# A decoder trunk's down projection as seven block products in three phases between the feed-forward tiles

## The reference, cut to what matters

```python
    x = layer_norm(ALPHA * x + merged @ w_out, ln1_g, ln1_b)
    f = (jax.nn.silu(x @ w_ff_gate) * (x @ w_ff_up)) @ w_ff_down
    x = layer_norm(ALPHA * x + f, ln2_g, ln2_b)
```

## Time and profile before

| what | value |
|---|---|
| three runs | 937.16, 937.13, 936.77 us; median 937.13 |
| span of the profiled execution | 935.2 us |
| TensorE busy | 921.6 us (99%) in 7307 matmuls |
| VectorE, ScalarE, GpSimd busy | 709.8, 423.3, 258.3 us |
| feed-forward quads | 575 to 786 us |
| down projection | 786 to 924 us |

### The profile page before, as it was taken

The page is one execution under the profiler, slowest core; times in us unless marked ns, Lnnn a source line. Parts: engine busy times, 40 slices in busy tenths (PEclk is TensorE's granted clock), DMA queues, the critical chain, the costliest instruction groups (busy, mean ns, idle before and its releaser), DMA issues.

```text
span 935.2 us, 18698 instructions
## 1 busy us (share of the span) xinstructions
PE 921.6 (99%) x7307; PEld 918.0 (98%) x7307; DVE 709.8 (76%) x1063; ACT 423.3 (45%) x682; POOL 258.3 (28%) x230
## 2 busy tenths in 40 slices
PE   9999999999999999999999999999999999999995
PEld 8999999999999999999999999999999999999995
DVE  2899999899869889877877699987878878321126
ACT  4422232326667534555544357555554557222223
POOL 4666565658200000000006441000000004443324
PEclk9999999999999999999999999999999999999998
DMA  8633233313436434432333321433334333422202
GB/s 237 193 88 86 84 100 90 89 58 91 144 115 220 164 111 115 114 88 83 108 102 113 94 66 47 120 106 90 90 95 123 96 90 104 145 86 85 79 2 96
DMA packets 169413, 98.29 MB, mean 105 GB/s; under 512 B 4954, under 2 KB 165506, under 8 KB 169361
## 3 DMA queue, kind: packets, MB, share of 16 engines
q1 hardware_dynamic: 167129, 96.66, 35.4%
q10 hardware_dynamic: 2232, 0.92, 0.4%
HBM read 89.94 MB, written 7.62 MB: 104 GB/s over the span
## 4 chain that ended last, share of the span: by engine, by line
PE 94%; DVE 3%; POOL 1%; DMA 1%; issue 0%; ACT 0%; SPq 0%; POOLq 0%; DVEq 0%
PE main L1323 49%; PE main L1484 27%; PE aux L1484 5%; PE aux L1323 4%; PE main L1556 4%; PE aux L1556 1%; PE main L1748 1%; PE aux L1309 1%; DMA x_tok<-in_x_prompt 1%; PE main L1359 1%; POOL r_tok L760 1%; DVE merged L2244 1%; DVE main L2241 0%; POOL r_tok L762 0%; DVE aux L2255 0%; PE aux L1699 0%
## 5 line engine op out<-in xcount | busy, mean ns | idle before, releaser
L644 POOL TENSOR_TENSOR w_lo<-raw,w_hi 128x1024 fp32r<-128x1024 f32 (+1 forms) x70 | 166.7, 2385 | 627.9 <-ACT w_hi L774 620.8
L774 ACT ACTIVATE w_hi<-raw 128x1024 fp32r<-128x1024 f32 x127 | 133.8, 1057 | 149.5 <-PE main L1323 114.9
L1323 PE MATMUL main<-x_hi,w_lo 128*128 128x272 f32 x752 | 155.8, 288 | 0.0
L1323 PE MATMUL main<-x_hi,w_hi 128*128 128x272 f32 x752 | 155.6, 288 | 0.0
L1323 PE MATMUL main<-x_lo,w_hi 128*128 128x272 f32 x752 | 155.1, 288 | 0.0
L1323 PEld LDWEIGHTS main<-x_hi,w_lo 128*128 128x128 f32 x752 | 118.1, 188 | 0.0
L1323 PEld LDWEIGHTS main<-x_lo,w_hi 128*128 128x128 f32 x752 | 118.1, 188 | 0.0
L1323 PEld LDWEIGHTS main<-x_hi,w_hi 128*128 128x128 f32 x752 | 117.4, 189 | 0.0
L1874 DVE SCALAR_TENSOR_TENSOR aux<-glu_pad,miscT,aux 128x512 f32<-128x512 f32 x112 | 75.1, 748 | 0.0
L2229 DVE SCALAR_TENSOR_TENSOR scr<-x_lo,main 128x544 f32<-128x544 f32 x6 | 4.3, 722 | 86.9 <-PE main L1323 86.9
L1323 PE MATMUL main<-y,w_hi 128*128 128x272 f32 x384 | 63.6, 287 | 0.0
(11 more groups left out here) (438 smaller groups left out, 2670.6 us busy)
## 6 DMA issues: line engine op xcount, KB each, us to landing
raw<-in_w_in SPq DMA_DIRECT2D x63, 512.0 KB, 4.2
raw<-in_w_ff_gate SPq DMA_DIRECT2D x22, 512.0 KB, 4.0
raw<-in_w_ff_up SPq DMA_DIRECT2D x22, 512.0 KB, 5.1
raw<-in_w_branch SPq DMA_DIRECT2D x32, 256.0 KB, 3.5
raw<-in_w_ff_down SPq DMA_DIRECT2D x16, 512.0 KB, 3.9
raw<-in_w_out SPq DMA_DIRECT2D x8, 512.0 KB, 3.9
raw<-in_w_ff_down SPq DMA_DIRECT2D x8, 384.0 KB, 3.3
kept_sums<-g_made_hi SPq DMA_DIRECT2D x4, 544.0 KB, 3.5
```

Of the source, the lines that this page charges most:

```text
L644: pool.tensor_tensor(w_lo[s][:, 0:n, :], raw[s][:, 0:n, :], w_hi[s][:, 0:n, :].bitcast(F32), ALU.subtract).then_inc(w_lo_ready, 1)
L774: act.activation(w_hi[s][:, :, :], raw[s][:, :, :], ACT.Copy).then_inc(w_hi_ready, 1)
L1323: mm = pe.matmul(ps[:, h, :], w[s][:, k, :], x[:, h * HALF:(h + 1) * HALF], start=(first and k == 0 and j == 0), stop=(last and k == n - 1 ...
```

## The change

The down projection is no longer a stage of its own. The 22 hidden chunks are taken as 11 pairs, in three phases of 4, 4 and 3 pairs. After the feed-forward quads 0 to 6 come four steps of phase 0 ("down", 0, o), after 7 to 14 four of phase 1, after 15 to 19 the last phase (list STEPS, 33 steps; step s in what follows is its index: 0 to 6, 7 to 10, 11 to 18, 19 to 22, 23 to 27, and 28 to 32 at the end). A down step makes two output tiles (2o and 2o + 1) from the pairs of its phase by the same seven products as a feed-forward quad: 4 chunks x 3 = 12 matmuls in each product of phases 0 and 1, 9 in phase 2. The blocks are a11, a12, a21, a22 of the hidden tiles (second index: even or odd chunk; first: rows 272 to 543 or 0 to 271) and their sums s1 to s4. In phase 2 only tiles 0 to 5 are done so; tiles 6 and 7 ("plain", steps 28 and 32) take 6 chunks x 3 x 2 matmuls each.

GpSimd makes for every pair the four sums (hid_sum) and the seven low parts (hid_low; eight in phase 2), each an operation of 272 columns, in the step after the pair is complete (steps 0, 2, 4, 6, 12, 14, 16, 18, 24, 26, and 27 and 28 for the last). ScalarE makes the high parts (hid_high) between its other work. The partial outputs are kept in merged, which ScalarE first scales by ALPHA (scale_x1, after steps 1 to 4): in every down step GpSimd adds the old value to each kept part (add_rows), VectorE's add_11, add_12 and add_22 write back to merged, and add_21 is a new one. The residual is thereby already in; the two operations of residual become one for the plain tiles (add_plain, residual_last) and none for the others. GpSimd no longer makes the low parts of the weights, except four in the last steps; VectorE does. The hardware loops over quads are written out flat. SP loads each tile of w_ff_down in two transfers and brings ln2_g and ln2_b ahead of the weights of step 31. Tiles are transposed in the order 6, 1, 0, 3, 2, 5, 4, 7.

The core of the diff (SP, GpSimd, ScalarE, TensorE, VectorE in turn):

```diff
+FIRST_PAIR, PAIRS = (0, 4, 8), (4, 4, 3)
+STEPS = ([("ff", q) for q in range(7)] + [("down", 0, o) for o in range(4)]
+         + [("ff", q) for q in range(7, 15)] + [("down", 1, o) for o in range(4)]
+         + [("ff", q) for q in range(15, KF - 2)] + [("plain", KD - 2)]
+         + [("down", 2, o) for o in range(3)] + [("plain", KD - 1)])
+S_LAST = len(STEPS) - 1
+S_PLAIN, S_END = STEPS.index(("plain", KD - 2)), STEPS.index(("down", 2, 2))
...
+            for s in range(S_LAST + 1):
+                kind, p = STEPS[s], s % 2
+                if s < 2:
+                    sp.wait_ge(w_lo_ready, U_FF + 2 * s + 2)
+                else:
+                    sp.wait_ge(left_lo_ready, s - 1)
+                    sp.wait_ge(right_lo_ready, quads(s - 2))
+                    sp.wait_ge(t4_ready, quads(s - 2))
+                if s == S_END:
+                    sp.wait_ge(p7_done, quads(S_PLAIN))
+                    for dst, name in ((g_row, "ln2_g"), (b_row, "ln2_b")):
+                        sp.dma_start(dst[:, :], i_[name].to_broadcast([P, D])).then_inc(row_vecs, 16)
...
-            with pool.Fori(0, KD // 4) as i:
-                for j in range(12):
-                    lo(i * 12 + (U_DOWN + j), j % RING, DOWN_SPLIT[j % 3])
...
+                a, b, op = {"s1": ("a21", "a22", ALU.add), "s2": ("s1", "a11", ALU.subtract),
+                            "s3": ("a11", "a21", ALU.subtract), "s4": ("a12", "s2", ALU.subtract)}[part]
...
+                pool.tensor_tensor(hid_f(part, ph, j), hid_f(a, ph, j), hid_f(b, ph, j), op)\
+                    .then_inc(hid_sum_ready, 1)
...
+            def pair_sums(ph, j):
+
+                both_made(ph, j, 0)
+                both_made(ph, j, 1)
+                hid_sum(ph, j, "s1")
+                hid_sum(ph, j, "s2")
+                hid_sum(ph, j, "s3")
+                hid_low(ph, j, "a11", "s3")
+                if ph == 2:
+                    hid_low(ph, j, "a21", "s3")
+                hid_sum(ph, j, "s4")
+                hid_low(ph, j, "s1", "s2")
+                hid_low(ph, j, "a12", "s4")
+                hid_low(ph, j, "s2", "s4")
+                hid_low(ph, j, "s3")
+                hid_low(ph, j, "s4")
+                hid_low(ph, j, "a22", "s1")
+
+            def add_rows(s):
+
+                if s == step_of("down", 0, 0):
+                    pool.wait_ge(x1_scaled, KD // 2)
+                for kept, rdy, where in ((kept_1, kept_1_ready, "11"), (kept_5, kept_5_ready, "22"),
+                                         (kept_2, kept_2_ready, "12")):
+                    pool.wait_ge(rdy, sums_to(s))
+                    pool.tensor_tensor(kept[:, :], kept[:, :], rows_of(s, where), ALU.add).then_inc(kept_added, 1)
...
+            for ph in range(2):
+                for j in range(PAIRS[ph]):
+                    pair_sums(ph, j)
+                for o in range(4):
+                    add_rows(step_of("down", ph, o))
+            pair_sums(2, 0)
+            pair_sums(2, 1)
+            both_made(2, 2, 0)
+            hid_sum(2, 2, "s3")
+            hid_low(2, 2, "a11")
+            hid_low(2, 2, "a21")
+            tile_made(KF - 1, 0)
+            hid_low(2, 2, "a12")
+            hid_low(2, 2, "s3")
+            tile_made(KF - 1, 1)
+            hid_sum(2, 2, "s1")
+            hid_sum(2, 2, "s2")
+            hid_low(2, 2, "s1", "s2")
+            hid_low(2, 2, "a22", "s1")
+            hid_sum(2, 2, "s4")
+            hid_low(2, 2, "s2", "s4")
+            hid_low(2, 2, "s4")
+            right_low(S_PLAIN + 2)
+            add_rows(S_PLAIN + 1)
+            left_low(S_PLAIN + 3)
+            right_low(S_PLAIN + 3)
+            add_rows(S_PLAIN + 2)
+            left_low(S_LAST)
+            add_rows(S_PLAIN + 3)
...
+                pair = pair_of(s - 1) if s else (0, 0)
+                left_high(s + 1)
+                keep_1(s)
+                if is_quad(s + 1):
+                    sum_high(s + 1, 0)
+                keep_5(s)
+                if is_quad(s + 1):
+                    right_high(s + 1)
+                if pair:
+                    hid_high(*pair, "a11")
+                    if pair[0] < 2:
+                        hid_high(*pair, "a12")
+                if is_ff(s - 1):
+                    silu_2(s - 1)
+                if is_quad(s + 1):
+                    sum_high(s + 1, 1)
+                keep_2(s)
+                if pair and pair[0] == 2:
+                    hid_high(*pair, "a21")
+                    hid_high(*pair, "a12")
+                if pair:
+                    hid_high(*pair, "a22")
+                    hid_high(*pair, "s1")
+                if is_quad(s + 1):
+                    sum_high(s + 1, 2)
+                if is_ff(s):
+                    silu_1(s)
+                if pair:
+                    hid_high(*pair, "s2")
+                    hid_high(*pair, "s3")
+                    hid_high(*pair, "s4")
...
+            for s in range(S_PLAIN - 1):
+                step(s)
+                if 1 <= s <= KD // 2:
+                    scale_x1(2 * s - 2)
...
+            s = S_PLAIN
+            left_high(s + 1)
+            hid_high(2, 2, "a12")
+            sum_high(s + 1, 0)
+            right_high(s + 1)
+            sum_high(s + 1, 1)
+            silu_2(s - 1)
+            hid_high(2, 2, "s1")
+            hid_high(2, 2, "a22")
+            hid_high(2, 2, "s2")
+            sum_high(s + 1, 2)
+            hid_high(2, 2, "s4")
             act.wait_ge(bn_zero, 1)
             act.activation(bn_rs[:, 0:1, 0:1], bn_mv[:, 0:1, 1:2], ACT.Sqrt, bias=EPS)
...
+            s = S_PLAIN + 1
+            keep_1(s)
+            keep_5(s)
+            left_high(s + 1)
+            sum_high(s + 1, 0)
+            right_high(s + 1)
+            keep_2(s)
+            sum_high(s + 1, 1)
+            sum_high(s + 1, 2)
...
+            for s in range(S_PLAIN):
+                product_1(s)
+                product_5(s)
+                if s:
+                    product_4(s - 1)
+                product_6(s)
+                product_2(s)
+                product_3(s)
+                product_7(s)
+
+            s, f0 = S_PLAIN, 2 * FIRST_PAIR[2]
+            pe.wait_ge(left_lo_ready, s + 1)
+            pe.wait_ge(hid_lo_ready, made(lo_order, 2, 1, "a22"))
+            for f in range(f0, f0 + 4):
+                first_plain(f, first=(f == f0))
+            product_4(s - 1)
+            pe.wait_ge(hid_lo_ready, made(lo_order, 2, 2, "a21"))
+            first_plain(f0 + 4)
+            s = S_PLAIN + 1
+            product_1(s)
+            product_2(s)
+            product_5(s)
+            pe.wait_ge(hid_lo_ready, made(lo_order, 2, 2, "a22"))
+            first_plain(f0 + 5, last=True).then_inc(plain_done, 1)
+            product_6(s)
+            product_3(s)
+            product_7(s)
...
+            def add_21(s):
+
+                rows_ = rows_of(s, "21")
+                ve.wait_ge(p4_done, quads(s))
+                ve.tensor_tensor(rows_, bank_of(s, "a"), rows_, ALU.add).then_inc(c21_ready, 1)
...
+            s = S_PLAIN + 1
+            two_sums(s + 1)
+            third_sum(s + 1)
+            sum_low(s + 1, 0)
+            add_11(s)
+            last_sum(s + 1)
+            sum_low(s + 1, 1)
+            left_low(s + 1)
+            add_plain()
+            sum_low(s + 1, 2)
+            add_12(s)
```

More of the change, by code:

```diff
@@ L257, in build @@
                 ("up_1", "up_2", "gate_1", "gate_2", "kept_1", "kept_2", "kept_5")))
[L259 to L274 removed]
+        HB = HALF * 4
@@ new lines, in made, with is_ff, is_quad, quads @@
+        def made(order, ph, j, part):
+            done = 0
+            for ph_ in range(ph + 1):
+                for j_ in range(PAIRS[ph_] if ph_ < ph else j):
+                    done += len(order(ph_, j_))
+            return done + order(ph, j).index(part) + 1
+        def is_ff(s):
+            return 0 <= s and STEPS[s][0] == "ff"
+        def is_quad(s):
+            return 0 <= s and STEPS[s][0] != "plain"
+        def quads(s):
+            return sum(is_quad(t) for t in range(s + 1))
@@ new lines, in scale_x1, with pair_of @@
+            def scale_x1(m):
+                if m == 0:
+                    act.wait_ge(x_sum_ready, 4)
+                    act.wait_ge(x1_lo_ready, 2 * KD)
+                part = merged[:, m:m + 2, :]
+                act.activation(part, part, ACT.Copy, scale=ALPHA).then_inc(x1_scaled, 1)
+            def pair_of(s):
+                if not is_ff(s) or STEPS[s][1] % 2 == 0:
+                    return None
+                g = STEPS[s][1] // 2 + 1
+                ph = sum(g >= k0 for k0 in FIRST_PAIR) - 1
+                return ph, g - FIRST_PAIR[ph]
@@ new lines, in _ @@
+            s = S_PLAIN + 1
+            keep_1(s)
+            keep_5(s)
+            left_high(s + 1)
+            sum_high(s + 1, 0)
+            right_high(s + 1)
+            keep_2(s)
+            sum_high(s + 1, 1)
+            sum_high(s + 1, 2)
+            s = S_PLAIN + 2
```

(51 more changed lines are left out.)

933 lines of the change are left out of this document (517 added, 416 removed).

## The result

The changed kernel takes 952.59 us (median of 4 runs, 951.73 to 954.0), the kernel before 937.14 (4 runs): 1.0167 times, with a 95% interval of 1.0153 to 1.0182. Forecast were 957 and slower. The profiled execution has a span of 952.2 us, 17.0 more than before.

A forecast was written before the change was run, and what follows sets the result against it. TensorE was taken to bound the feed-forward and down projection, but not the end. Span 935.2 less 1.8 (saving left after the end part) plus 22.0 (turns) gave 955.4; with 1.9 to the runs' median, 957 us, range 936 to 970.

The forecast's parts named there:

- The saving: Down projection: 933 matmuls instead of 1056, 123 fewer at 0.1255 us each, 15.4 us less.
- The edits at nothing: Weight transfers, row vectors, scale_x1, flat loops and VectorE's work in down steps were all priced at no cost.
- The turns: GpSimd and two-SBUF-input VectorE operations alternate, each turn costing VectorE about 0.6 us; 22.0 us in all.
- phase 0: Cost of GpSimd turns in this phase: 4.4 + 1.6 + 1.6 + 3.6 = 11.2 us, the 4.4 at step 0.
- phase 1: Cost of GpSimd turns in this phase: 0.3 + 1.6 + 1.6 + 3.6 = 7.1 us.
- the steps to the end of 27: Phase 2's turns: 0.9 for its first pair, 1.3 for ScalarE's s3 copy waiting before keep_2; 2.2 us.
- Rival D: Feed-forward and down steps: half the GpSimd and VectorE turns collide, costing 11 us, giving 946; chance 0.23.
- The Trainium skill's rule: A two-SBUF-input VectorE operation and a GpSimd operation hold a shared port pair exclusively; the other fully blocks.
- The end part: After product 7 of step 27: waits sum to 7.2 us; without the lock the saving of 15.4 becomes 1.8.
- C: ScalarE becomes the bound: s4 late from GpSimd delays keep_1 before product 6, 14 us on top, 971; chance 0.17.
- A: The lock hardly bites, only the end part costs: 935.3, on the edge between faster and the same; chance 0.10.
- B: The saving arrives, the end part's waits absent too: 921.7, or 929.5 with half of it; chance 0.10.

The follow-up runs named there:

- e1: The changed kernel with the sums and low parts of ten of the eleven pairs moved from GpSimd to VectorE: 941.46 us, 1.0044.
- b_two: The kernel before plus 114 GpSimd subtractions of two 128x272 SBUF tiles in the feed-forward, onto a scratch tile: 948.87 us, 1.0122.
- b_set: The kernel before plus 114 GpSimd memsets of a 128x272 scratch tile in the feed-forward: 938.36 us, 1.0012.
- all: The changed kernel with every pair on VectorE, pair (0,0) one step later, square root behind rows(4), steps 29 and 30 reordered: 934.96 us, 0.9976.
- all3: all with the last stretch reordered, three waits mended and the last four weight parts moved from GpSimd to VectorE: 930.61 us, 0.9928.

## Why the forecast was right, and where its numbers were off

**The saving** is as counted: 7307 matmuls before, 7184 after, 123 less, and where nothing waits 72 of them take 9.04 us as in the earlier trace rows.

**The edits at nothing.** No wait of TensorE behind 575 us names a transfer. scale_x1 did cost, though no wait names it. ScalarE before product 6 of step 3, which waited 1.02 us for keep_1 (the last row):

```profile
613.77 0.43 ACT L1420 ACTIVATE x_hi<-h_f 128x272 fp32r<-128x272 f32 x1 [1.13 <-POOL h_f L888]
614.10 1.10 ACT L1428 ACTIVATE merged<-merged 128x1088 f32<-128x1088 f32 x1
...
616.05 0.38 ACT L1383 ACTIVATE kept<-main 128x272 f32<-128x272 f32 x1
```

The second row is scale_x1, between a hid_high that waited for GpSimd's s4 and keep_1. Step 5 has the same order and waits 0.93. In phase 1 the pairs come the same way, without scale_x1, and product 6 waits nowhere. No run takes scale_x1 out by itself.

**The turns** are shown, not only argued: GpSimd subtractions alone lengthen VectorE's two-input operations in the kernel before, memsets do not, and taking the pairs off GpSimd gives 11.1 us back. The size was too large. The sum had 20.5 us for the 28 steps; measured are 13.4, and 1.5 of clock. By term: phase 0 has 7.7 for 11.2, since step 0 lost some 1.9 (0.59 + 0.70 + 0.57) for 4.4; phase 1 has 4.0 for 7.1; the steps to the end of 27 have 1.8 for 2.2. Not all of the 7.7 are turns: the 0.59 of step 0 stays in e1, and scale_x1 has its part in the 1.02 and 0.93. The failed assumption is the one turn for every GpSimd operation: I laid them out with both queues always full. The two-input groups of the 28 steps are together about 59 us longer than before, over 137 GpSimd operations 0.43 each, and b_two gives 0.39; a collision costs 0.58, about as put, so about 0.7 of the operations have one. Rival D, with half the collisions, was off by 6.6 us on the other side (946).

**The Trainium skill's rule** (SBUF — State Buffer, the two separate sides) is borne out by b_two and e1 as to which operations block each other. The section limits it, for VectorE operations with two SBUF inputs, to GpSimd operations that read SBUF; by that a memset takes no turn, and b_set agrees (VectorE's mean 0.686 us beside 114 memsets, 0.685 without). The row at 798.30 that passed may be one of the third that does; no run shows why they pass.

**The end part** was placed wait by wait. Measured: product 5 of step 29 waits 1.61 (forecast 0.75, plus the 1.5 put down to turns), product 6 1.90 (1.9), product 1 of step 30 4.00 (3.65), by the queue named. These are the rows behind the last:

```profile
901.53 1.84 POOL L939 TENSOR_TENSOR w_lo<-raw,w_hi 128x768 fp32r<-128x768 f32 x1 [2.45 <-ACT w_hi L1376]
903.33 2.50 POOL L924 TENSOR_TENSOR kept<-kept,merged 128x272 f32<-128x272 f32 x3
```

```profile
904.19 0.44 DVE L2752 TENSOR_TENSOR merged<-aux,kept 128x272 f32<-128x272 f32 x1 [2.87 <-POOL kept L924]
904.54 0.67 DVE L2680 TENSOR_TENSOR w_sum<-raw,w_sum 128x384 f32<-128x384 f32 x1
905.14 1.11 DVE L2686 TENSOR_TENSOR w_sum_lo<-w_sum,w_sum_hi 128x384 fp32r<-128x384 f32 x1
906.17 0.95 DVE L2732 TENSOR_TENSOR w_lo<-raw,w_hi 128x768 fp32r<-128x768 f32 x1
```

right_low, add_rows, add_11, and left_low(30) last in the queue. Together 47.4 us were forecast from the end of step 27 to the last statistics; it is 49.7, and 2.2 of the difference is the clock that fell in the wait of 4.00.

**The sum:** 955.4 of span less 7.1 for the turns and with 3.7 for the clock is 952.0, and the span is 952.2. The profiled run itself took 954.0, 1.8 above its span as before, but it is the slowest of the four, and the median lies 1.4 below it. That the forecast came within 5 us is in part luck: turns put 7.1 too high were partly made up by a clock that the sum did not have.

**The rivals.** C (ScalarE) has its mechanism in the trace, but not its size: keep_1 is the releaser in 4.7 us of waits. 1.9 of them are at the table load; before the others (1.02, 0.93 and 0.85, steps 3, 5 and 27) ScalarE had waited 1.13, 1.13 and 2.41 us for GpSimd's s4, with left_high and keep_1 behind, as C says. That is 2.8 us and not 14. A gave 935.3 as the time without turns, and all, with no pair on GpSimd, came to 935.0 with its own small stalls. B, the other side, had the whole saving arrive once the end part is free of waits. all3 is nearly that: 39.4 us from the end of step 27 to the last statistics (873.06 to 912.49), where the sum without its waits had 38.7, and TensorE stands still for 2.0 us in all between 583 us and the tail. Still it is 6.7 us faster, not 15.4. TensorE's last transposes of the kernel before, and of all3 in the second fence, show why:

```profile
925.44 0.44 PE L1728 MATMUL aux<-ident,scr 128*128 128x128 f32 x2 [1.05 <-DVE scr L2517]
```

```profile
918.68 0.69 PE L2071 MATMUL aux<-ident,merged 128*128 128x128 f32 x2 [5.43 <-DVE merged L2981]
```

TensorE is through with its products 11.2 us earlier (913.2 for 924.4), the last statistics begin 5.6 us earlier (912.49 for 918.12 in the earlier trace rows). Before, 6.3 us of products ran beside the tail; now 0.8 do, and the statistics of two row tiles stand in the tail's chain, as forecast. Of the 11.2 us that TensorE gained, 5.6 end there.

## What to carry to other kernels

When work is moved to GpSimd because it stands idle, price it at what it takes from VectorE: here 0.58 us per collision (0.39 to 0.43 for each GpSimd operation) for a 272-column operation that VectorE does itself in 0.35, and 1.65 for a 768-column one of 0.87. In a list that is full, take away the operation that many wait behind first, and look for the next wait in the same list before counting the gain: here most edits in the full list of the end part gave back part of their gain one step on. Of the 15.4 us in matmuls 6.7 arrived, after 22 us of waits and half clock had been taken out of the first version. The releaser that a wait names is only the last link; what stood ahead of it in its engine's list has to be read too. A stage in which TensorE is the bound shows its saving only if the tail behind it does not hang on something else.
